# Last norm of a one-core hybrid decoder layer: a reordered finish, with the left output halves on GpSimd and ScalarE

## Chip, cores and metric

The kernel runs on one core of a Trainium2 chip. The metric is the device time in microseconds (us) of one execution. Engines are called by their names in the profile: PE (TensorE matmul), PEld (TensorE weight load), DVE (VectorE), ACT (ScalarE), POOL (GpSimd), SP (the engine that issues most DMAs).

## What is computed

One decoder layer over 512 tokens of width 1024: two mixing branches, a cross-attention, a mixture of 64 experts of which each token takes 8, and a last RMS norm. Only the end matters here:

```python
def rmsnorm(x, g):
    xf = x.astype(jnp.float32)
    y = xf * lax.rsqrt(jnp.mean(xf * xf, axis=-1, keepdims=True) + EPS)
    return (y * g.astype(jnp.float32)).astype(x.dtype)

    h = h + moe(rmsnorm(h, g_ffn[l]), ...)
return rmsnorm(h, g_final)
```

In `moe`, a token's output is the sum of its 8 expert rows, each times its gate, plus a shared expert's row (already in `h` when the end begins).

## The kernel before

All arithmetic is in float32. The 512 tokens are four tiles (`NT` = 4) of 128 partitions; `h[:, i, :]` in SBUF is tile `i`, 1024 wide. The expert rounds (44 of them) fill most of the time: weights stream from memory, PE multiplies, and POOL writes the rows of each round to a buffer in memory by indirect DMA.

The end begins when the last rounds are written. SP loads the 8 expert rows of each token back, as 16 transfers of 1024 KB: a "row pair" for each `q` of 0 to 3 and each tile `i` (`load_row_pairs`, L700 to L709). The pairs lie in the weight buffers that have come free (`ring`, `dw`, `z`). Each tile's 1024 columns are then summed in two halves by two engines:

- The right half (columns 512 to 1023) on PE: `sum_right_halves` (L1290) adds `h` and the 8 rows, each times a diagonal matrix of gates, into a PSUM bank `ps[:, i, :]`. The last pair of a tile raises `s_prs`. Between `q` = 1 and `q` = 2 PE also spreads the last norm's weight over the partitions (L1309), and ACT copies it to `gf` in SBUF (L1644).
- The left half (columns 0 to 511) on DVE: `add_rows` (L2286) for `q` 0 to 2 and `sum_last` (L2312) for `q` = 3, two `scalar_tensor_tensor` operations each, in place in `h`. `sum_last(i)` raises `s_red`.

ACT squares each half with a sum over the columns (L1647 left, L1649 right), and after tiles 1 and 3 takes a square root (`roots`, L1343) of the mean that DVE has made (`tile_squares`, L2294: an add, and `mean_square` at L1680). DVE makes the inverse root with one correction step (`tile_roots`, `inverse_root` at L1690: a reciprocal and four small operations, each waited for by `link`). `scale(i)` (L2304) multiplies both halves of tile `i` by the inverse root and by `gf`; each half raises `s_fin`. SP stores the eight halves, 256 KB each, in the order left 0, right 0, left 1, right 1, and so on (L736 to L740), each after its own count of `s_fin`, and waits for all of them at the end.

The order of each engine's work is its program order; nothing is reordered at run time. DVE's order at the end is written out in `sum_and_finish` (L2328 to L2338). POOL has nothing to do after its last indirect DMA. The tiles `h`, `z`, `ring`, `tok` and `st` lie in SBUF, `ps` in PSUM.

Of the kernel before, what the change touches and what calls it, by code (L numbers as in the profile page):

```python
# [21 lines left out]
ALU = mybir.AluOpType  # L22
ACT = mybir.ActivationFunctionType
# [6 lines left out]
D = 1024  # L30
S = 512
NT = S // P
# [14 lines left out]
EPS = 1e-6  # L47
# [11 lines left out]
PI_MAX = 3.1415925  # L59


C_ID, C_ONE, C_CAUSAL, C_FREQ, C_SLOT, C_BEFORE, C_FOLD, C_KEY = 0, 128, 192, 320, 352, 356, 420, 484
NCONST = 485
QW, NQ = 32, 4
FIXED, FULL, THREE = 4, 8, 24
NBUF = 6
# [84 lines left out]
def shape_constants():  # L151

    c = np.zeros((P, NCONST), np.float32)
    c[:, C_ID:C_ID + P] = np.eye(P)
    c[:, C_ONE:C_ONE + NE] = 1.0
    q, k = np.arange(P)[:, None], np.arange(P)[None, :]
    c[:, C_CAUSAL:C_CAUSAL + P] = np.where(k <= q, 0.0, -BIG)
    c[:, C_FREQ:C_FREQ + DQ // 2] = 10000.0 ** (-np.arange(0, DQ, 2) / DQ)
    for i in range(NT):
        c[:, C_SLOT + i] = S * TOPK - TOPK * (P * i + np.arange(P))  # L160
    a, b = np.arange(NG)[:, None], np.arange(NG)[None, :]
    c[:, C_BEFORE:C_BEFORE + NG * NG] = (b < a).astype(np.float32).ravel()
    c[:, C_FOLD:C_FOLD + NE] = np.tile(np.eye(NE), (2, 1))
    e = np.arange(NE)
    key = np.where(e < FIXED, -S * NE * 3 * (1 + e), NE - 1 - e)
    c[0:NE, C_KEY] = key
    late = np.zeros((P, NLATE), np.float32)
    for q in range(NQ):
        late[:, L_RANK + q * NR:L_RANK + (q + 1) * NR] = [RANK_AT[UNITS[r][1][q]] for r in BY_COL]
    late[:, L_KEY:L_KEY + NE] = key  # L170
    late[0:NE, L_EXP:L_EXP + QW] = e[:, None]
    return np.concatenate([c, late], axis=1)
# [11 lines left out]
def hybrid_layer(nc, t, consts, out):  # L184
# [5 lines left out]
    def sem(name):  # L190
        return ctx.enter_context(nc.semaphore(name))


    h = sb("h", [P, NT, D])
    tok = sb("tok", [P, NT * D])
    act_t = sb("act_t", [P, NC_D * S])
    z = sb("z", [P, NT * 2048])
    dw = sb("dw", [P, 3, 2048])
    ring = sb("ring", [P, 4, 6144])
    cst = sb("cst", [P, NCONST])  # L200
    pcol = sb("pcol", [P, NROWS])
    gcat = sb("gcat", [P, NC_D])
    st = sb("st", [P, 96])
# [13 lines left out]
    def view(base, off, *dims):  # L217

        n = int(np.prod(dims))
        v = base[:, off:off + n]  # L220
        names = "abcd"[:len(dims)]
        if len(dims) == 1:
            return v
        return v.rearrange("p (%s) -> p %s" % (" ".join(names), " ".join(names)),
                           **{k: d for k, d in zip(names, dims)})

    K = 256
# [43 lines left out]
    st2 = sb("st2", [P, 64])  # L271
# [63 lines left out]
    s_sq = sem("squares_ready")  # L335
    s_var = sem("variance_ready")
    s_sd = sem("deviation_ready")
    s_dev = sem("deviations_of_x_then_moe_ready")
    s_tf = sem("turned_filled")
    s_tea = sem("turned_evac_act")  # L340
    s_tev = sem("turned_evac_dve")
# [41 lines left out]
    s_oe = sem("attn_out_evac")  # L383
    s_osq = sem("attn_squares_ready")
    s_gin = sem("gelu_input_then_inner_ready")
    s_gst = sem("gelu_squares_ready")
    s_th = sem("tanh_ready")
    s_yg = sem("gelu_ready")
    s_ygt = sem("gelu_turned")
    s_yge = sem("gelu_turned_evac")  # L390
    s_gl = sem("gate_filled")
    s_sg = sem("gate_sigmoid_ready")
    s_y3 = sem("gated_ready")
    s_cat = sem("branches_ready")
    s_memn = sem("mem_normed")
# [55 lines left out]
    s_yl = [sem(f"rows_loaded{i}") for i in range(10)]  # L451
    s_red = sem("tile_rows_summed")
    s_prs = sem("half_rows_summed_pe")
    s_fin = sem("output_ready")
    s_out = sem("output_stored")


# [15 lines left out]
    tp = view(z, 0, NT, D)  # L473
    scr = view(z, 16 * K, 12, NT * NE)
    grow = view(ya, 0, D)
    rbias = view(ya, D, NE)
    wr = view(ya, D + NE, NC_D, NE)
    tv, ts_, row_of = view(tok, 3 * D, S), view(tok, 3 * D + S, SLOTS), view(tok, 3 * D + S + SLOTS, NE)
# [29 lines left out]
    yo = [view(z, (8 + b * 4) * K, D) for b in range(2)]  # L508

    gf_row = z[0:1, 0:D]  # L510
    gf, gf_spread = z[:, D:2 * D], ps[:, 6:8, :].rearrange("p a b -> p (a b)")
    LOADED = [[0, 0, 1, 1], [2, 2, 3, 3], [4, 4, 5, 5], [6, 7, 8, 9]]
    OF_LOAD = [sum(row.count(n) for row in LOADED) for n in range(10)]
# [81 lines left out]
    def _(sp):  # L595
# [140 lines left out]
        for i in range(NT):  # L736
            for n in range(2):
                cols = slice(n * 512, (n + 1) * 512)
                sp.wait_ge(s_fin, 2 * i + n + 1)
                sp.dma_start(out[0, i * P:(i + 1) * P, cols], h[:, i, cols]).then_inc(s_out, 16)  # L740
        sp.wait_ge(s_out, 16 * 2 * NT)

# [583 lines left out]
    def _(act):  # L1326
# [16 lines left out]
        def roots(n, a, b):  # L1343

            act.wait_ge(s_var, n)
            act.activation(st[:, b], st[:, a], ACT.Sqrt).then_inc(s_sd, 1)
# [288 lines left out]
        def norm_squares():  # L1635

            act.wait_ge(s_gk, NT * TOPK + 1)
            for q in range(4):
                for i in range(NT):
                    for k in range(2):  # L1640
                        act.activation(gate_diagonal(q, i, k), ident, ACT.Copy, scale=gate_of(q, i, k)).then_inc(s_dg, 1)
            act.activation(st2[:, 44:45], st2[:, 0:1], ACT.Sqrt)
            act.wait_ge(s_prs, 1)
            act.activation(gf, gf_spread, ACT.Copy).then_inc(s_dg, 1)  # L1644
            for i in range(NT):
                act.wait_ge(s_red, i + 1)
                act.activation(tok3[:, i, 0:512], h[:, i, 0:512], ACT.Square, accum_out=st[:, i:i + 1]).then_inc(s_sq, 1)  # L1647
                act.wait_ge(s_prs, 1 + i + 1)
                act.activation(tok3[:, i, 512:D], ps[:, i, :], ACT.Square, accum_out=st[:, 4 + i:5 + i]).then_inc(s_sq, 1)  # L1649
                if i % 2:  # L1650
                    roots(7 + i // 2, slice(i - 1, i + 1), slice(8 + i - 1, 8 + i + 1))

        with act.If(slots_needed(act) < 1):
            norm_squares()
# [7 lines left out]
    def _(dve):  # L1662
# [17 lines left out]
        def mean_square(var, width):  # L1680

            link(dve.tensor_scalar(var, var, 1.0 / width, EPS, ALU.mult, ALU.add))
            dve.sem_inc(s_var, 1)
# [610 lines left out]
        def tile_squares(a, b):  # L2294

            dve.wait_ge(s_sq, 18 + 2 * b)
            link(add(st[:, a:b], st[:, a:b], st[:, 4 + a:4 + b]))
            mean_square(st[:, a:b], D)

        def tile_roots(a, b):  # L2300

            inverse_root(7 + a // 2, st[:, a:b], st[:, 8 + a:8 + b], st2[:, a:b])

        def scale(i):  # L2304

            dve.wait_ge(s_dg, 2 * NT * 4 + 1)
            for n in range(2):
                cols = slice(n * 512, (n + 1) * 512)
                dve.scalar_tensor_tensor(out=h[:, i, cols], in0=ps[:, i, :] if n else h[:, i, cols], scalar=st2[:, i:i + 1],
                                         in1=gf[:, cols], op0=ALU.mult, op1=ALU.mult).then_inc(s_fin, 1)  # L2310

        def sum_last(i):  # L2312

# [8 lines left out]
        def sum_and_finish(loads):  # L2322

            dve.wait_ge(s_gk, NT * TOPK + 1)
            for q in range(3):
                for i in range(NT):
                    add_rows(q, i, loads, slice(0, 512))
            for i in range(3):  # L2328
                sum_last(i)
            tile_squares(0, 2)  # L2330
            tile_roots(0, 2)
            sum_last(3)
            scale(0)
            tile_squares(2, 4)
            scale(1)
            tile_roots(2, 4)
            scale(2)
            scale(3)  # L2338
# [25 lines left out]
    def _(pool):  # L2364
# [98 lines left out]
        with needs_passes(pool):  # L2463
            all_scattered(NR)
            with pool.Fori(0, PASSES) as p:
                pool.wait_ge(s_tab, p + 3)
                pool.sem_inc(s_zero, 1)
                one_pass(p)
            pool.sem_inc(s_rows, 1)

    ctx.close()

# [17 lines left out]
```

## Time and profile before

| | us |
|---|---|
| time, median of 3 runs | 1126.96 |
| lowest and highest run | 1123.72, 1128.65 |
| span of the profiled execution, first to last instruction | 1122.3 |
| PE busy | 1072.1 (96%) |
| DVE busy | 392.8 (35%) |
| ACT busy | 233.1 (21%) |
| POOL busy | 121.7 (11%) |

The span is of one execution, recorded by the profiler on the core. A busy share is an average over the whole span; the end, from about 1080 us on, is read from its own stretch. Positions in the trace are us from the start of the span. Rows of consecutive like instructions are merged in a timeline (x2, x3), and pipelined neighbours can overlap by up to 0.1 us.

### The profile page before, as it was taken

The numbers are of one execution on the slowest core, as the hardware profiler recorded it, in microseconds if no ns is written. First come the engines' busy times: TensorE is split into PE (matmuls) and PEld (weight loads), VectorE is DVE, ScalarE is ACT, GpSimd is POOL, SyncE is SP. The second block draws the span as 40 slices with busy tenths as digits, with TensorE's granted clock in tenths as the row PEclk, the third lists the DMA queues.
The fourth block names the chain that finished last, engine by engine and source line by source line (L and its number), as shares of the span: only waits on it lengthen the run. The fifth ranks groups of instructions, "written<-read, shape, count | busy, mean of one in ns | idle before, by whom it ended". The sixth has DMA issues, their size and how long they took to land.

```text
span 1122.3 us, 13366 instructions
## 1 busy us (share of the span) xinstructions
PE 1072.1 (96%) x5091; PEld 520.6 (46%) x5091; DVE 392.8 (35%) x924; ACT 233.1 (21%) x528; POOL 121.7 (11%) x187
## 2 busy tenths in 40 slices
PE   7999999989999999988899999999999998999996
PEld 4444687764444484443444433333344343443332
DVE  1894764553220040069322122122122121111157
ACT  4311523454111050031011111111111111111142
POOL 3000000000000000000211212211212211121100
PEclk9999999999999999999999999999999999999998
DMA  7225334221262502235699999999999999999997
GB/s 220 79 78 118 92 118 115 84 75 38 75 271 73 195 25 72 75 138 230 234 410 418 419 422 420 420 421 420 422 419 421 420 420 422 421 419 422 419 408 286
DMA packets 77346, 298.81 MB, mean 266 GB/s; under 512 B 20343, under 2 KB 23708, under 8 KB 50653
## 3 DMA queue, kind: packets, MB, share of 16 engines
q1 hardware_dynamic: 64386, 264.29, 60.1%
q0 software_dynamic: 12672, 33.57, 7.7%
q8 instruction: 42, 0.69, 0.2%
q14 instruction: 28, 0.22, 0.1%
q10 hardware_dynamic: 218, 0.04, 0.0%
HBM read 280.04 MB, written 27.39 MB: 274 GB/s over the span
## 4 chain that ended last, share of the span: by engine, by line
PE 87%; DVE 7%; ACT 2%; DMA 2%; issue 1%; DVEq 0%; SPq 0%; ACTq 0%
PE ps L1211 27%; PE ps L771 25%; PE ps L1227 14%; PE ps L1193 4%; PE ps L902 3%; PE ps L915 2%; PE ps L1300 2%; PE ps L1235 1%; DVE tok L2180 1%; DMA dw<-in_wv_x 1%; DVE tok L2177 1%; PE ps L1061 1%; PE ps L1080 1%; PE ps L951 1%; PE ps L752 1%
## 5 line engine op out<-in xcount | busy, mean ns | idle before, releaser
L1211 PE MATMUL ps<-ring,z 128*32 128x512 f32 (+2 forms) x1024 | 275.6, 594 | 0.7 <-DVE z L2228 0.5
L771 PE MATMUL ps<-dw,act_t 128*128 128x512 f32 x576 | 249.1, 593 | 1.3 <-ACT act_t L1518 1.0
L771 PEld LDWEIGHTS ps<-dw,act_t 128*128 128x128 f32 x576 | 108.8, 190 | 135.4 <-issue 133.5
L1227 PE MATMUL ps<-ring,act_t 128*32 128x512 f32 (+2 forms) x512 | 144.3, 607 | 4.5 <-issue 3.7
L1211 PEld LDWEIGHTS ps<-ring,z 128*32 128x32 f32 (+2 forms) x1024 | 87.7, 131 | 110.3 <-issue 108.2
L1211 PE MATMUL ps<-dw,z 128*64 128x512 f32 (+2 forms) x256 | 99.0, 594 | 2.1 <-issue 1.1
L1211 PE MATMUL ps<-z 128*32 128x512 f32 (+2 forms) x320 | 98.9, 594 | 0.0
L1604 ACT ACTIVATE tok<-ps 128x256 f32<-128x256 f32 x44 | 16.9, 383 | 299.8 <-PE ps L1211 299.8
L2208 DVE COPY z<-ps 128x512 f32<-128x512 f32 x44 | 30.4, 692 | 121.1 <-PE ps L1227 121.1
L1227 PEld LDWEIGHTS ps<-ring,act_t 128*32 128x32 f32 (+2 forms) x512 | 42.9, 133 | 55.1 <-issue 53.2
L1672 DVE TENSOR_TENSOR tok<-tok,ps 128x256 f32<-128x256 f32 x22 | 9.3, 421 | 151.2 <-ACT tok L1604 151.2
L1672 DVE TENSOR_TENSOR act_t<-tok,ps 128x256 f32<-128x256 f32 x22 | 9.3, 421 | 147.6 <-ACT tok L1604 147.6
L2374 POOL COPY ixb<-tabs 128x1 uint32<-128x1 uint32 x88 | 17.0, 193 | 375.2 <-DVE z L2208 361.9
L2443 POOL MEMSET act_t<- 128x1024 f32 x1 | 1.0, 952 | 510.1 <-PE ps L771 510.1
L771 PE MATMUL ps<-act_t,dw 128*128 128x512 f32 x128 | 55.2, 593 | 0.9 <-ACT act_t L1355 0.9
L1600 ACT ACTIVATE z<-ps 128x512 f32<-128x512 f32 x44 | 26.3, 597 | 137.9 <-PE ps L1227 137.9
L1227 PE MATMUL ps<-act_t 128*64 128x512 f32 (+2 forms) x128 | 50.9, 597 | 0.0
L1227 PE MATMUL ps<-dw,act_t 128*32 128x512 f32 (+2 forms) x160 | 50.9, 596 | 0.0
L2418 POOL DMA_INDIRECT expert_rows<-z,ixb x44 | 44.7, 1015 | 36.2 <-POOL ixb L2374 36.2
L1211 PEld LDWEIGHTS ps<-dw,z 128*64 128x64 f32 (+2 forms) x256 | 29.4, 132 | 33.7 <-issue 33.1
L1211 PEld LDWEIGHTS ps<-z 128*32 128x32 f32 (+2 forms) x320 | 29.9, 127 | 32.0 <-issue 31.3
L1193 PEld LDWEIGHTS ps<-cst,tok 128*128 128x128 f32 x264 | 32.5, 193 | 24.7 <-issue 24.7
(326 smaller groups left out, 1220.9 us busy)
## 6 DMA issues: line engine op xcount, KB each, us to landing
ring<-in_w_gate SPq DMA_DIRECT2D x40, 1024.0 KB
ring<-in_w_up SPq DMA_DIRECT2D x40, 1024.0 KB
ring<-in_w_down SPq DMA_DIRECT2D x40, 1024.0 KB, 26.8
dw<-in_w_gate SPq DMA_DIRECT2D x12, 1024.0 KB
dw<-in_w_up SPq DMA_DIRECT2D x12, 1024.0 KB
act_t<-in_w_down SPq DMA_DIRECT2D x12, 1024.0 KB, 24.6
z<-in_w_gate SPq DMA_DIRECT2D x12, 1024.0 KB, 19.9
z<-in_w_up SPq DMA_DIRECT2D x12, 1024.0 KB, 23.6
```

The lines of the kernel that those rows point to most:

```text
L771: ins = pe.matmul(ps[0:m, bank0 + j, 0:n], lhs(w, q * 4 + c4, c4, j), rhs(w, q * 4 + c4, c4, j), start=(q == 0 and c4 == 0), stop=(q == le ...
L902: ins = pe.matmul(ps[:, bank, 0:MEM], w4(dw[:, i % 3, :])[:, c4, j * P:(j + 1) * P], memt[:, hf * 4 + c4, :], start=(hf == 0 and c4 == 0), ...
L915: ins = pe.matmul(ps[:, bank, 0:256], memt[:, hf * 4 + c4, m * P:(m + 1) * P], w4(dw[:, i % 3, :])[:, c4, n * 256:(n + 1) * 256], start=(h ...
L1193: ins = pe.transpose(ps[:, c // 4, (c % 4) * P:(c % 4 + 1) * P], xg[r % 4][:, c:D:NC_D], ident)
L1211: ins = pe.matmul(ps[rows, 2 + r % 2, :], xtt[r % 2][:, c, rows], ring_wgu(BUF[x])[:, :, c, :], start=(c == 0), stop=(c == NC_D - 1))
L1227: ins = pe.matmul(ps[rows, 5 + n, :], htt[r % 2][:, c, rows], ring_wd(BUF[x])[:, c, n * 512:(n + 1) * 512], start=(c == 0), stop=(c == 1))
L1300: ins = pe.matmul(ps[:, i, :], gate_diagonal(q, i, k), row_pair(q, i)[:, k, 512:D], start=False, stop=(q == 3 and k == 1))
L1600: act.activation(yo[j % 2][:, 0:512], ps[:, 5, :], ACT.Copy).then_inc(e_yea, 1)
L1672: return dve.tensor_tensor(o, a, b, ALU.mult)
L2208: dve.tensor_copy(yo[j % 2][:, 512:D], ps[:, 6, :]).then_inc(e_yev, 1)
L2374: pool.tensor_copy(ixb[:, b:b + 1], tabs[:, which, col:col + 1] if isinstance(col, int) else tabs[:, which, bass.ds(col, 1)]).then_inc(s_p ...
L2418: pool.indirect_dma_start(yr, bass.IndirectOffsetOnAxis(ap=ixb[:, b:b + 1], axis=0), yo[r % 2], None, bounds_check=last_row, oob_is_err=Fa ...
```

## The change

Only the end of the kernel changes, and a constant that it needs.

1. DVE's order: `sum_last(3)` is put ahead of `tile_roots(0, 2)`, and `scale(1)` ahead of `tile_squares(2, 4)`.
2. `scale(i)` on DVE makes the right half alone. The left half becomes two steps. POOL multiplies `h[:, i, 0:512]` by `gf` into `left_products` as soon as `sum_last(i)` is done. ACT multiplies the product by the inverse root into `h`, all four tiles after its second square root.
3. `tile_squares`: the count that ACT's square root waits for is raised after the add; the mean is made beside it, and ACT takes scale and bias into the root (the new constant column `C_EPS`). `tile_roots`: a reciprocal and three operations in place of a reciprocal and four.
4. SP waits for ACT's count for left halves (`s_finl`) and DVE's count for right halves (`s_fin`). The order of the stores stays.

```diff
+c[:, C_EPS] = EPS          (NCONST 485 -> 486)
+    s_root, s_lp, s_finl = s_dev, s_gst, s_sg
+    left_products = view(z, 8 * K, NT, 512)
@@ SP
-                sp.wait_ge(s_fin, 2 * i + n + 1)
+                sp.wait_ge(*((s_fin, i + 1) if n else (s_finl, NT + i + 1)))
                 sp.dma_start(out[0, i * P:(i + 1) * P, cols], h[:, i, cols]).then_inc(s_out, 16)
@@ ACT, norm_squares
                 if i % 2:
-                    roots(7 + i // 2, slice(i - 1, i + 1), slice(8 + i - 1, 8 + i + 1))
+                    act.wait_ge(s_var, 7 + i // 2)
+                    act.activation(st[:, 8 + i - 1:8 + i + 1], st[:, i - 1:i + 1], ACT.Sqrt, scale=1.0 / D, bias=eps
+                                   ).then_inc(s_sd, 1)
+            for i in range(NT):
+                act.wait_ge(s_root, 3 + i // 2)
+                act.wait_ge(s_lp, NT + i + 1)
+                act.activation(h[:, i, 0:512], left_products[:, i, :], ACT.Copy, scale=st2[:, i:i + 1]).then_inc(s_finl, 1)
@@ DVE
             link(add(st[:, a:b], st[:, a:b], st[:, 4 + a:4 + b]))
-            mean_square(st[:, a:b], D)
+            dve.sem_inc(s_var, 1)
+            dve.tensor_scalar(st2[:, 40 + a:40 + b], st[:, a:b], 1.0 / D, EPS, ALU.mult, ALU.add)
         def tile_roots(a, b):
-            inverse_root(7 + a // 2, st[:, a:b], st[:, 8 + a:8 + b], st2[:, a:b])
+            r, near, mean = st2[:, a:b], st2[:, 32 + a:32 + b], st2[:, 40 + a:40 + b]
+            dve.wait_ge(s_sd, 7 + a // 2)
+            link(dve.reciprocal(r, st[:, 8 + a:8 + b]))
+            link(dve.scalar_tensor_tensor(out=near, in0=r, scalar=-0.5, in1=r, op0=ALU.mult, op1=ALU.mult))
+            link(mul(near, near, mean))
+            dve.scalar_tensor_tensor(out=r, in0=near, scalar=1.5, in1=r, op0=ALU.add, op1=ALU.mult).then_inc(s_root, 1)
         def scale(i):
             dve.wait_ge(s_dg, 2 * NT * 4 + 1)
-            for n in range(2):
-                cols = slice(n * 512, (n + 1) * 512)
-                dve.scalar_tensor_tensor(out=h[:, i, cols], in0=ps[:, i, :] if n else h[:, i, cols], scalar=st2[:, i:i + 1],
-                                         in1=gf[:, cols], op0=ALU.mult, op1=ALU.mult).then_inc(s_fin, 1)
+            dve.wait_ge(s_root, 3 + i // 2)
+            dve.scalar_tensor_tensor(out=h[:, i, 512:D], in0=ps[:, i, :], scalar=st2[:, i:i + 1], in1=gf[:, 512:D],
+                                     op0=ALU.mult, op1=ALU.mult).then_inc(s_fin, 1)
@@ DVE, sum_and_finish
             tile_squares(0, 2)
+            sum_last(3)
             tile_roots(0, 2)
-            sum_last(3)
             scale(0)
+            scale(1)
             tile_squares(2, 4)
-            scale(1)
             tile_roots(2, 4)
@@ POOL, at its end
+        pool.wait_ge(s_dg, 2 * NT * 4 + 1)
+        for i in range(NT):
+            pool.wait_ge(s_red, i + 1)
+            pool.tensor_tensor(left_products[:, i, :], h[:, i, 0:512], gf[:, 0:512], ALU.mult).then_inc(s_lp, 1)
```

## Rows read from the trace of the kernel before

**Rows 1.** The page: the chain that ended last, share of the span by engine.

```profile
PE 87%; DVE 7%; ACT 2%; DMA 2%; issue 1%; DVEq 0%; SPq 0%; ACTq 0%
```

**Rows 2.** Chain of work that ended last, from 1080 us: start, us, what.

```profile
1108.93 0.70 ACT tok L1649 x2
...
1112.91 0.72 ACT tok L1647 x2
...
1118.47 1.32 DVE h L2309 x2
```

**Rows 3.** Timeline, DVE: start, us, line op out<-in count [idle before <-releaser].

```profile
1103.69 1.54 DVE L2316 SCALAR_TENSOR_TENSOR h<-z,st,h 128x512 f32<-128x512 f32 x2
1105.44 1.54 DVE L2316 SCALAR_TENSOR_TENSOR h<-z,st,h 128x512 f32<-128x512 f32 x2 [0.21 <-DMA z<-expert_rows]
1107.93 1.54 DVE L2316 SCALAR_TENSOR_TENSOR h<-ring,st,h 128x512 f32<-128x512 f32 x2 [0.95 <-DMA ring<-expert_rows]
1109.65 0.16 DVE L1675 TENSOR_TENSOR st<-st 128x2 f32<-128x2 f32 x1 [0.18 <-ACT tok L1649]
...
1110.34 0.17 DVE L1694 RECIPROCAL st<-st 128x2 f32<-128x2 f32 x1 [0.33 <-ACT st L1346]
...
1111.33 1.54 DVE L2316 SCALAR_TENSOR_TENSOR h<-ring,st,h 128x512 f32<-128x512 f32 x2
1112.79 0.75 DVE L2309 SCALAR_TENSOR_TENSOR h<-h,st,z 128x512 f32<-128x512 f32 x1
1113.45 0.75 DVE L2309 SCALAR_TENSOR_TENSOR h<-ps,st,z 128x512 f32<-128x512 f32 x1
...
1116.08 0.15 DVE L1694 RECIPROCAL st<-st 128x2 f32<-128x2 f32 x1
```

**Rows 4.** Timeline, ACT, the square root and tile 3's squares.

```profile
1110.11 0.20 ACT L1346 ACTIVATE st<-st 128x2 f32<-128x2 f32 x1 [0.49 <-DVEq L1683]
...
1112.91 0.63 ACT L1647 ACTIVATE tok<-h 128x512 f32<-128x512 f32 x1 [1.41 <-DVE h L2316]
...
1113.54 0.58 ACT L1649 ACTIVATE tok<-ps 128x512 f32<-128x512 f32 x1
...
1114.01 0.19 ACT L1649 ACTIVATION_READ_ACCUMULATOR tok<-ps 128x1 f32 x1
```

**Rows 5.** Timeline, PEld: the wait for the last row pair.

```profile
1110.36 0.30 PEld L1300 LDWEIGHTS ps<-ring,act_t 128*128 128x128 f32 x2 [0.58 <-DMA ring<-expert_rows]
```

**Rows 6.** Timeline, SP: the eight stores, from first to last issue.

```profile
1113.56 6.58 SPq L740 DMA_DIRECT2D out<-h  x8
```

**Rows 7.** Windows: stretch, us, busy by engine, PEclk, DMA share, GB/s.

```profile
1114.00:1114.50 0.50, 0.00 (x0) 0.00 (x0) 0.43 (x3) 0.20 (x2) 0.00 (x0) 1.00 0.36 106
1118.50:1119.00 0.50, 0.00 (x0) 0.00 (x0) 0.50 (x1) 0.00 (x0) 0.00 (x0) 0.50 0.67 254
1120.00:1120.50 0.50, 0.00 (x0) 0.00 (x0) 0.00 (x0) 0.00 (x0) 0.00 (x0) 0.50 1.05 385
1121.00:1121.50 0.50, 0.00 (x0) 0.00 (x0) 0.00 (x0) 0.00 (x0) 0.00 (x0) 0.50 0.84 324
```

**Rows 8.** Timeline of 1079.8 to 1080.7 us, DVE and POOL.

```profile
1079.82 1.53 DVE L2291 SCALAR_TENSOR_TENSOR h<-ring,st,h 128x512 f32<-128x512 f32 x2
1080.04 0.56 POOL L2374 COPY ixb<-tabs 128x1 uint32<-128x1 uint32 x1 [2.97 <-DVE z L2208]
```

**Rows 9.** All 88 POOL copies of line 2374: ns min/median/max, first and last start.

```profile
L2374 POOL COPY ixb<-tabs x88: 177/183/562, 536.4 to 1080.0; 128x1 uint32<-128x1 uint32 x88
```

**Rows 10.** Timeline from 3 us: POOL and DVE at the kernel's start.

```profile
0.75 3.51 POOL L2366 MEMSET ring<- 128x4096 f32 x1 [0.29 <-POOLq L2478]
...
3.24 1.09 DVE L1728 COPY ring<-st 16x128 f32<-16x128 f32 x1 [3.24 <-DMA st<-in_log_dt]
```

**Rows 11.** DVE copies of 128x32: ns min/median/max, first and last start.

```profile
L1778 DVE COPY ring<-pw x8: 172/173/181, 38.2 to 38.8; 128x32 f32<-128x32 f32 x8
```

**Rows 12.** Groups by line, POOL: busy, mean ns of one, idle before.

```profile
L2443 POOL MEMSET act_t<- 128x1024 f32 x1 | 1.0, 952 | 510.1 <-PE ps L771 510.1
```

More of the change, by code:

```diff
@@ L59 @@
 PI_MAX = 3.1415925
-C_ID, C_ONE, C_CAUSAL, C_FREQ, C_SLOT, C_BEFORE, C_FOLD, C_KEY = 0, 128, 192, 320, 352, 356, 420, 484
-NCONST = 485
+C_ID, C_ONE, C_CAUSAL, C_FREQ, C_SLOT, C_BEFORE, C_FOLD, C_KEY, C_EPS = 0, 128, 192, 320, 352, 356, 420, 484, 485
+NCONST = 486
 QW, NQ = 32, 4
@@ L166, in shape_constants @@
     c[0:NE, C_KEY] = key
+    c[:, C_EPS] = EPS
     late = np.zeros((P, NLATE), np.float32)
@@ L337, in hybrid_layer @@
     s_sd = sem("deviation_ready")
-    s_dev = sem("deviations_of_x_then_moe_ready")
+    s_dev = sem("deviations_of_x_then_moe_then_output_ready")
     s_tf = sem("turned_filled")
@@ L385, in hybrid_layer @@
     s_gin = sem("gelu_input_then_inner_ready")
-    s_gst = sem("gelu_squares_ready")
+    s_gst = sem("gelu_squares_then_left_products_ready")
     s_th = sem("tanh_ready")
@@ L391, in hybrid_layer @@
     s_gl = sem("gate_filled")
-    s_sg = sem("gate_sigmoid_ready")
+    s_sg = sem("gate_sigmoid_then_left_output_ready")
     s_y3 = sem("gated_ready")
@@ L453, in hybrid_layer @@
     s_prs = sem("half_rows_summed_pe")
-    s_fin = sem("output_ready")
+    s_fin = sem("right_output_ready")
     s_out = sem("output_stored")
@@ L475, in hybrid_layer @@
     grow = view(ya, 0, D)
+    eps = cst[:, C_EPS:C_EPS + 1]
     rbias = view(ya, D, NE)
```

## The prediction

> **What bounds the kernel now.** I read the chain that ended last first. Over the whole span it is PE's, 87% of it [rows 1], and none of that is touched: up to about 1109 us PE multiplies while row pairs arrive. The change can act only on what follows. There the chain leaves PE at ACT's square of tile 1's right half, goes through tile 3's sum and squares, and ends in DVE's scalings [rows 2]. The last ends at 1118.47 + 1.32 = 1119.79 us. The span ends at 1122.3, so 2.5 us are the last stores.
>
> Next the DMA share in short windows, as the end is a store problem too. The first store is issued at 1113.56 [rows 6]; its half-microsecond window is busy for 0.36 x 0.5 = 0.18 us [rows 7], so data starts to flow at 1114.32, 0.76 us after the issue. The last four halves (left 2 to right 3) flow in one piece from 1119.00 - 0.67 x 0.5 = 1118.66 to 1121.00 + 0.84 x 0.5 = 1121.42, at a DMA share of 1.05 in the middle [rows 7]: 2.76 us for four, 0.69 us for each. DVE makes a half in 1113.45 - 1112.79 = 0.66 us [rows 3]. The two rates are nearly equal, so stores can hardly catch up on a late start. From the last byte (1121.42) to the end of the span it is 0.88 us. Eight stores back to back therefore cost 0.8 (issue to flow) + 8 x 0.69 + 0.88 = 7.2 us from the first issue. Before, 8.7 us lay between (1113.56 to 1122.3), with gaps of about 1.3 us.
>
> **What the first store will wait for.** SP's order stays: left 0 comes first, and everything stands behind it, right halves that have long been done too. Left 0 now comes from ACT, whose program has it behind the second square root. So the start of all stores hangs on tile 3. First without any contention:
> - The last row pair is there at 1110.36 [rows 5]. Before, DVE made tiles 0 and 1's roots first and summed tile 3 from 1111.33 to 1112.88. Now it sums from 1110.37: done at 1111.91, 0.97 us sooner.
> - The roots of tiles 0 and 1 follow. Five linked operations took 1111.33 - 1110.34 = 0.99 us, 0.2 each [rows 3]; four take 0.8: until 1112.71.
> - Right 0 and right 1, 0.66 us each, occupy DVE until 1114.05. Meanwhile ACT squares tile 3: from 1111.93, 1114.20 - 1112.91 = 1.29 us as before [rows 4], until 1113.22. It then waits for DVE, since the add of tiles 2 and 3 stands behind right 1. This is a wait that the new order makes: 0.8 us in which tile 3's squares lie ready.
> - Add 0.16 us, the count, square root 0.20: before, add start to root start was 1110.11 - 1109.65 = 0.46 us [rows 3, 4]; without the mean between, 0.26. The root ends at about 1114.52.
> - ACT's scaling of left 0. Its nearest row is the square of a left half in SBUF, 0.63 us [rows 4]; it ends at 1115.15.
>
> The first issue is then at 1115.17, against 1113.56 before: 1.6 us later. ACT needs about 0.6 us for each left half and a tile's two stores take 1.38, so the other left halves are in time (left 2 waits also for roots at about 1115.35, and is done before 1117). Right 3 is done at about 1116.75, 3 us sooner than before. Stores then run without a gap: 1115.17 + 7.2 = 1122.37. That is 0.1 us against the 1122.3 of before. All that compute gains goes into the later start.
>
> **What POOL's products cost.** They cost nothing on POOL, which is idle, and the fourth is wanted only some 2 us after left 0 is scaled. But POOL and DVE get in each other's way. One of POOL's 88 copies took 562 ns, median 183 [rows 9]. It started at 1080.04 and ended at 1080.60, just as the first of two DVE row sums ended, an operation with two SBUF inputs (1079.82 + 1.53/2 = 1080.58) [rows 8]. The other way round, a DVE copy of 16x128 took 1.09 us while POOL's memset ran, and ended at 4.33 where the memset ended at 4.26 [rows 10]; a DVE copy of 128x32 takes 0.17 [rows 11]. So each engine was seen waiting for the other's whole instruction. By the Trainium skill (SBUF — State Buffer, SBUF: two separate sides), the pair of ports that the two share is an exclusive lock: a GpSimd operation that reads SBUF and a VectorE operation with two SBUF inputs shut each other out for a full instruction. Both rows agree, though this pair of kinds with POOL ahead is not shown.
>
> I count as shut out what is of the kind of the row sums in [rows 8], with two inputs in SBUF: `sum_last`, the adds and three of the four root steps. The right halves read one input from PSUM and are counted free; so are the reciprocal and the mean, which have one input (if they are shut out too, as the copy of [rows 10], which also has one, that is up to 0.2 us more). The length d of a product stands in no row. POOL's nearest rows are memsets, which write only: 0.95 us for 128x1024 [rows 12], 3.51 for 128x4096 [rows 10], thus 0.83 ns an element. Lower bound: 512 elements at that rate with the fixed tenth, 0.5 us. Upper: three streams (two read, one written) of 512, 1.4 us. I take 0.95, two streams, the memset of 1024. (The Trainium skill, GPSIMD Engine Reference, Performance versus the Vector engine, has 4497 ns for 2048 elements of a two-input operation; by that an estimate of 1.1 us, and the sum below would be 0.6 us more.)
>
> With d = 0.95 and 0.14 us from a DVE end to a POOL start (before POOL's copy of 1080.04, DVE's previous operation ends at 1079.90):
> - product 0 holds until 1106.32, so tile 1's sum runs 1106.34 to 1107.88 instead of 1105.44 to 1106.98; this is hidden, as tile 2's rows arrive at 1107.93 [rows 3];
> - product 1 falls between the two operations of tile 2's sum: done 1110.40 instead of 1109.47;
> - product 2 starts behind the add at 1110.58 and holds until 1111.53; tile 3's sum ends at 1113.09 instead of 1111.91: 1.18 us;
> - product 3 starts at 1113.23, behind the reciprocal, and holds until 1114.18; the three other root steps follow: roots done 1114.79 instead of 1112.71, 2.08 us in all.
>
> Everything behind moves by these 2.08: first issue 1117.25, end 1124.45. Forecast: 1122.3 + 2.1 = 1124.4 for the span. The median of the runs (1126.96) stands 4.7 us above the profiled span, the fastest run 1.4; I carry the difference to the median over: 1126.96 + 2.1 = 1129.1 us. With d = 0.5 it is +0.5, with 1.4 +3.9 (roughly 3.9 us per us of d).
>
> The 486th constant column is 0.2% more of one early load; at most 0.02 us.
>
> **Rivals.**
> - No lock between these kinds. For: the rows show one pair of kinds in each direction, neither with POOL reading and ahead. Against: both show it. Then the sum without contention holds, 1122.4 for the span: 1127.0 us.
> - Not slower, and faster: compute bounds the end, not the stores. Place: SP's stores; they would have to flow quicker than 0.69 us each, or left 0 sooner. Then right 3 at 1116.75, plus 2.5 us: 1119.2, a gain of 3.1, 1123.9 us. Against: a share of 1.05 in the last burst [rows 7], and program order. It decides only where eight stores take under 2.4 us in all after 1115.17.
> - Clearly slower: products are long. From d = 0.95 + (5.6 - 2.1)/3.9 = 1.85 us on the loss is over 0.5% (1132.6 us); with d = 3, about 1137. Against: twice the memset of 1024 elements for half the elements.
>
> **Chances.** Forecast (lock, d 0.5 to 1.4) 0.58; no lock 0.24; compute-bound gain 0.07; long products 0.05; something outside the end, such as another course of the weight stream, 0.06. About 0.5% (5.6 us) is what a measurement can tell from no change: the three runs alone spread over 4.9 us. The whole stretch that changes is little longer, so within 0.5% holds 0.87. Over 0.5% slower: 0.09 (long products and the upper end of the forecast with the runs' spread). Over 0.5% faster: 0.04. Range: from 1124.0, the compute-bound case and the lower runs of no lock, to 1131.5, the forecast's upper bound (1130.9) with some spread.
>
> **What would show it.** Right: right 3 scaled well before its store; first store issue at about 1117.2, later than 1113.56, and then a DMA share near 1 without gaps for 5.5 us; DVE's tile sums showing gaps or long operations where POOL's products lie; POOL products of 0.5 to 1.4 us. Lock wrong: tile 3's sum ends at 1111.9 beside a running product, first issue 1115.2. Store bound wrong: gaps between stores with ACT late. The prediction fails if products take over 1.85 us, or if the time before 1105 us moves.

## The result, and the profile after

The changed kernel is a little slower: ratio to the kernel before 1.0027, 95% interval 1.0014 to 1.0040. Over 20 runs each, the medians are 1125.85 us and 1122.62 us. 0.27% of 1122.62 is 3.0 us (1.6 to 4.5).

The page of the changed kernel has the same shape; the chain's shares answer [rows 1]:

```profile
span 1122.6 us, 13377 instructions
...
PE 1072.9 (96%) x5091; PEld 520.8 (46%) x5091; DVE 393.3 (35%) x918; ACT 235.8 (21%) x532; POOL 127.7 (11%) x191
...
PE 87%; DVE 5%; DMA 3%; ACT 2%; issue 1%; SPq 0%; ACTq 0%; POOL 0%; POOLq 0%; DVEq 0%
```

The two spans, 1122.3 and 1122.6 us, hardly differ, and this is misleading: in the profiled execution of the changed kernel the whole end began 2.6 us sooner, since the streams of row pairs vary that much from one execution to the next. A common mark is needed. I take the start of DVE's sum of tile 1, which waits for that tile's last rows in every trace but follows no step of the change: 1105.44 before [rows 3], 1102.86 after. From this mark to the end of the span it is 16.86 us before and 19.74 after: 2.88 us longer, which is what the ratio says. The mark itself is good to about 0.35 us: two traces of one kernel differ by that much (below). The reason is PE, whose right halves come early or late against DVE's rows, so that DVE's add of tiles 0 and 1 starts 3.9 to 4.5 us after the mark in the traces where no product holds it up.

DVE's timeline of the changed kernel, which answers [rows 3]:

```profile
1101.09 1.54 DVE L2331 SCALAR_TENSOR_TENSOR h<-z,st,h 128x512 f32<-128x512 f32 x2
1102.86 2.53 DVE L2331 SCALAR_TENSOR_TENSOR h<-z,st,h 128x512 f32<-128x512 f32 x2 [0.22 <-DMA z<-expert_rows]
1105.34 2.43 DVE L2331 SCALAR_TENSOR_TENSOR h<-ring,st,h 128x512 f32<-128x512 f32 x2
1107.69 0.15 DVE L1685 TENSOR_TENSOR st<-st 128x2 f32<-128x2 f32 x1
1107.99 1.15 DVE L2309 TENSOR_SCALAR st<-st 128x2 f32<-128x2 f32 x1 [0.15 <-DVE st L1685]
1109.05 1.53 DVE L2331 SCALAR_TENSOR_TENSOR h<-ring,st,h 128x512 f32<-128x512 f32 x2
1110.49 0.16 DVE L2315 RECIPROCAL st<-st 128x2 f32<-128x2 f32 x1
1110.69 1.25 DVE L2316 SCALAR_TENSOR_TENSOR st<-st 128x2 f32<-128x2 f32 x1
...
1112.44 1.41 DVE L2324 SCALAR_TENSOR_TENSOR h<-ps,st,z 128x512 f32<-128x512 f32 x2
...
1115.21 1.41 DVE L2324 SCALAR_TENSOR_TENSOR h<-ps,st,z 128x512 f32<-128x512 f32 x2
```

POOL's timeline of the same stretch, which has no counterpart before:

```profile
1102.79 1.26 POOL L2488 TENSOR_TENSOR z<-h,z 128x512 f32<-128x512 f32 x1 [22.79 <-DVE h L2331]
1105.46 1.75 POOL L2488 TENSOR_TENSOR z<-h,z 128x512 f32<-128x512 f32 x1 [1.41 <-DVE h L2331]
1107.84 1.27 POOL L2488 TENSOR_TENSOR z<-h,z 128x512 f32<-128x512 f32 x1 [0.63 <-DVE h L2331]
1110.65 1.27 POOL L2488 TENSOR_TENSOR z<-h,z 128x512 f32<-128x512 f32 x1 [1.54 <-DVE h L2331]
```

Lay the two side by side. I say that POOL holds a DVE operation, or that a lock lies between them, where one stands still until the other is done. A product takes 1.26 us. The first starts at 1102.79, just ahead of tile 1's sum; the sum takes 2.53 us where 1.54 is its length. The second is asked for while the first operation of tile 2's sum runs: the product itself grows to 1.75 us (it waits for that operation), and the sum's second operation then waits for the product (2.43). The third holds the mean of tiles 0 and 1, a `TENSOR_SCALAR` of two columns: 1.15 us where 0.17 was. The fourth holds the second root step: 1.25 us where 0.16 was. The right halves from PSUM keep 1.41 us for two, but no product runs beside them here; the run with two of four products puts one there.

The chain that ended last shows the same places, and the ScalarE step that the stores wait for:

```profile
1107.99 1.15 DVE st L2309
...
1110.69 1.26 DVE st L2316
...
1114.21 0.93 ACT h L1661 x2
```

The stores (SP's timeline, then windows with DMA share and GB/s as the last two columns), which answer [rows 6, 7]:

```profile
1114.94 4.99 SPq L744 DMA_DIRECT2D out<-h  x8
```

```profile
1115.50:1116.00 0.50, 0.00 (x0) 0.00 (x0) 0.50 (x2) 0.50 (x2) 0.00 (x0) 0.50 0.40 152
1118.00:1118.50 0.50, 0.00 (x0) 0.00 (x0) 0.00 (x0) 0.00 (x0) 0.00 (x0) 0.50 1.01 389
1121.00:1121.50 0.50, 0.00 (x0) 0.00 (x0) 0.00 (x0) 0.00 (x0) 0.00 (x0) 0.50 0.56 213
```

The last half is computed at 1115.21 + 1.41 = 1116.62, but data flows from 1115.80 (1116.00 - 0.40 x 0.5) to 1121.28 (1121.00 + 0.56 x 0.5) without a gap: 5.48 us for eight halves. Computing ends 6.0 us before the span does; in the kernel before it was 2.5.

1121.28 is where the full flow ends, not the last byte. Windows of what follows, first after, then before:

```profile
1121.30:1121.80 0.50, 0.00 (x0) 0.00 (x0) 0.00 (x0) 0.00 (x0) 0.00 (x0) 0.50 0.09 33
1121.80:1121.90 0.10, 0.00 (x0) 0.00 (x0) 0.00 (x0) 0.00 (x0) 0.00 (x0) 0.50 0.01 0
1121.90:1122.60 0.70, 0.00 (x0) 0.00 (x0) 0.00 (x0) 0.00 (x0) 0.00 (x0) 0.50 0.00 0
```

```profile
1121.50:1121.60 0.10, 0.00 (x0) 0.00 (x0) 0.00 (x0) 0.00 (x0) 0.00 (x0) 0.50 0.02 0
1121.60:1122.30 0.70, 0.00 (x0) 0.00 (x0) 0.00 (x0) 0.00 (x0) 0.00 (x0) 0.50 0.00 0
```

In the changed kernel a trickle of packets of the stores' queue goes on until 1121.87, from 1121.4 on a packet every 0.08 us, where the share is near 1 in the full flow; from there to the end of the span it is 0.73 us. In the kernel before the last packet lies at 1121.55, just behind the full flow (1121.42), and the rest is 0.75 us.

### The profile page after: what moved, and what is told of

Read it like the earlier page. It is cut to its first block, busy times and chain, and to the rows that moved or that the text cites. A ratio compares the mean times of both kernels' runs of the same rounds, so it can differ in the third digit from the quotient of the medians.

```text
span 1122.6 us, 13377 instructions
## 1 busy us (share of the span) xinstructions
PE 1072.9 (96%) x5091; PEld 520.8 (46%) x5091; DVE 393.3 (35%) x918; ACT 235.8 (21%) x532; POOL 127.7 (11%) x191
## 4 chain that ended last, share of the span: by engine, by line
PE 87%; DVE 5%; DMA 3%; ACT 2%; issue 1%; SPq 0%; ACTq 0%; POOL 0%; POOLq 0%; DVEq 0%
PE ps L1215 27%; PE ps L775 27%; PE ps L1231 14%; PE ps L1197 4%; PE ps L906 3%; PE ps L919 2%; PE ps L1239 1%; DMA z<-expert_rows 1%; PE ps L756 1%; DVE tok L2190 1%; DVE tok L2187 1%; PE ps L1065 1%; PE ps L955 1%; PE ps L1084 1%; DMA dw<-in_wv_x 1%
```

## The experiments

The theory: (a) POOL's products and DVE's operations shut each other out (the lock), which delays left 0; (b) the end is then set by eight stores in a row behind their late start. The rivals: the loss comes from the new order alone; computing sets the end. Some runs leave out, shorten or replace the products, others store only half of each half: their output is not the layer's, and only their times are used.

All results in one table. "Offset" is the time in the trace from the mark (start of tile 1's sum on DVE), first to the first store's issue and then to the end of the span; its difference to the kernel before (16.86) stands beside the ratio from the timed runs, each with 95% interval.

| kernel | ratio to before | first issue | end | end against before |
|---|---|---|---|---|
| before | | 8.12 | 16.86 | |
| changed | 1.0027 (1.0014 to 1.0040) | 12.08 | 19.74 | +2.88 |
| no products | 1.0007 (0.9996 to 1.0019) | 9.74 | 17.19 | +0.33 |
| before, with products | 1.0020 (1.0005 to 1.0035) | 9.81 | 18.88 | +2.02 |
| left 0 and 1 ahead of the second root | 1.0017 (1.0003 to 1.0031) | 10.22 | 17.96 | +1.10 |
| the same without products | 1.0005 (0.9990 to 1.0019) | 8.53 | 16.89 | +0.03 |
| products of 256 columns | 1.0013 (1.0000 to 1.0027) | 10.54 | 18.11 | +1.25 |
| changed, stores of 256 columns | 1.0011 (0.9994 to 1.0029) | 12.07 | 17.65 | +0.79 |
| before, stores of 256 columns | 0.9994 (0.9978 to 1.0009) | 7.79 | 16.14 | -0.72 |
| two of four products | 0.9998 (0.9979 to 1.0018) | 6.28 | 15.75 | -1.11 |
| two of four, again | 1.0004 (0.9983 to 1.0025) | 6.80 | 16.10 | -0.76 |
| two of four, squares first | 0.9988 (0.9965 to 1.0011) | 6.86 | 16.18 | -0.68 |
| memsets for products | 1.0000 (0.9971 to 1.0028) | 9.74 | 17.27 | +0.41 |
| copies for products | 1.0000 (0.9976 to 1.0024) | 10.13 | 17.79 | +0.93 |

0.1% is 1.1 us. The intervals are as wide as most effects here; the offsets carry the readings, and every offset lies within its ratio's interval.

**Without the products.**

```diff
-            pool.tensor_tensor(left_products[:, i, :], h[:, i, 0:512], gf[:, 0:512], ALU.mult).then_inc(s_lp, 1)
-                act.wait_ge(s_lp, NT + i + 1)
-                act.activation(h[:, i, 0:512], left_products[:, i, :], ACT.Copy, ...)
+                act.activation(h[:, i, 0:512], h[:, i, 0:512], ACT.Copy, ...)
```

> The changed kernel without GpSimd's four products; ScalarE scales the left half of h itself, so the weight of the last norm is left out of the left output halves. Lock theory: the long VectorE records (1.75 and 1.64 us where 0.78 was before, 1.15 and 1.26 where 0.17) are gone, tile 3's left sum ends 1.55 us after its rows are there, the first store is issued 4.8 us after that arrival, eight stores take 7.2 to 7.7 us from there; the time is 3 us under the changed kernel, ratio to the kernel before 0.999 to 1.001. Rival (the loss comes from the order alone, GpSimd costs nothing): time as the changed kernel, ratio 1.0027. Rival (compute bounds the end): 3 us under the kernel before, 0.997.

DVE's timeline of this run:

```profile
1105.21 1.54 DVE L2330 SCALAR_TENSOR_TENSOR h<-z,st,h 128x512 f32<-128x512 f32 x2 [0.22 <-DMA z<-expert_rows]
1107.70 1.54 DVE L2330 SCALAR_TENSOR_TENSOR h<-ring,st,h 128x512 f32<-128x512 f32 x2 [0.94 <-DMA ring<-expert_rows]
1109.54 0.16 DVE L1684 TENSOR_TENSOR st<-st 128x2 f32<-128x2 f32 x1 [0.30 <-ACT tok L1653]
```

Every long record is gone, the first issue comes 2.34 us sooner (12.08 to 9.74), the end 2.55. So the products cause the long records and most of the loss; the order alone is no explanation, since it leaves 0.33 us. Nor is there the gain of the compute-bound rival: all that the change saves in computing is lost to the later start of the stores, as the next runs show.

**The kernel before, with the products beside it.** POOL's four products are added to the kernel before; nothing uses them.

```diff
+        pool.wait_ge(s_dg, 2 * NT * 4 + 1)
+        for i in range(NT):
+            pool.wait_ge(s_red, i + 1)
+            pool.tensor_tensor(left_products[:, i, :], h[:, i, 0:512], gf[:, 0:512], ALU.mult).then_inc(s_gst, 1)
@@ DVE, scale
+            dve.wait_ge(s_gst, NT + i + 1)
```

> The kernel before with the four GpSimd products beside it; their results are used by nothing, VectorE only waits for product i before it scales tile i in place. Lock theory: each product of 1.26 us stretches a VectorE operation with two SBUF inputs by about a product's rest; product 0 is hidden up to 0.3 us, the others cost 0.5 to 1.2 us each: 2 to 3.5 us slower than before, ratio 1.002 to 1.003. Rival (GpSimd costs nothing): ratio 1.000, every row sum of VectorE 0.75 us long.

2.2 us by the ratio, 2.02 by the offset. In the old order, too, the products by themselves cost about as much as the whole change lost (2.88). Their hold falls on the same kinds: DVE's timeline has the mean of two columns at 1.26 us, and the add of tiles 2 and 3 at 0.44:

```profile
1110.43 1.26 DVE L1683 TENSOR_SCALAR st<-st 128x2 f32<-128x2 f32 x1
...
1115.91 0.44 DVE L1676 TENSOR_TENSOR st<-st 128x2 f32<-128x2 f32 x1
```

**Left halves of tiles 0 and 1 ahead of the second root.**

```diff
@@ ACT, behind tile 3's squares, ahead of the second root
+                if i == 3:
+                    for m in range(2):
+                        act.wait_ge(s_root, 3 + m // 2)
+                        act.wait_ge(s_lp, NT + m + 1)
+                        act.activation(h[:, m, 0:512], left_products[:, m, :], ACT.Copy, scale=st2[:, m:m + 1]).then_inc(s_finl, 1)
```

> The changed kernel, but ScalarE scales the left halves of tiles 0 and 1 ahead of the second square root instead of behind it. Store theory (the start of the first store sets the end): left 0 is done 0.65 us after the first roots instead of 2.5 us after them, the first issue comes 1.9 us sooner, and as the stores then run without a gap the time falls by up to 1.9 us against the changed kernel: ratio to the kernel before 1.001. The second root moves by at most 0.3 us. Rival (the last computed half sets the end): no gain or a loss up to 0.3 us, ratio 1.0027.

First issue 1.86 us sooner, end 1.78 sooner, with the last half computed as late as in the changed kernel (right 3 at 1118.37, which is 13.73 after the mark, against 13.76). The start of the stores sets the end, not the last computed half.

**The same without products.** Both edits together.

> Both at once: no GpSimd products (the last norm's weight left out of the left output halves) and the left halves of tiles 0 and 1 scaled ahead of the second square root. Lock and store theory: the gains add, 4.9 us under the changed kernel and 1.9 us under the kernel before, ratio 0.998; the first store is issued 3.0 us after the last rows are there. Rival (stores do not bound): as the run without products alone.

The expectation was missed. The end is 0.30 us sooner than without products alone, not 1.9. The first issue gained 1.21, not 1.9: without the lock the first roots are ready at 1111.63, while ACT squares tile 3 until 1112.30. And the stores no longer ran in one piece (windows, DMA share second to last):

```profile
1114.00:1115.00 1.00, 0.00 (x0) 0.00 (x0) 0.78 (x5) 0.37 (x1) 0.00 (x0) 1.00 0.97 365
1115.00:1115.50 0.50, 0.00 (x0) 0.00 (x0) 0.50 (x2) 0.50 (x2) 0.00 (x0) 1.00 0.50 176
1115.50:1116.00 0.50, 0.00 (x0) 0.00 (x0) 0.50 (x1) 0.46 (x1) 0.00 (x0) 0.70 0.13 37
1116.00:1117.00 1.00, 0.00 (x0) 0.00 (x0) 0.12 (x1) 0.00 (x0) 0.00 (x0) 0.50 0.98 369
```

SP's timeline has the issue of the third store, left 1, at 1.61 us, where 0.45 is the median of the eight:

```profile
1113.89 1.61 SPq L744 DMA_DIRECT2D out<-h  x1
```

So a gap of 0.7 us opened in the stream. It wasn't computing that was late: left 1 was done at 1112.30 + 1.32 = 1113.62, and the fourth store, right 1, done at 1113.16, was issued only at 1115.55, behind the long issue. Why one issue takes so long stays open; the longest of the eight is 0.34 to 1.61 us over these traces, and a gap shows only where the stores have nothing queued.

**Products of 256 columns.**

```diff
-            pool.tensor_tensor(left_products[:, i, :], h[:, i, 0:512], gf[:, 0:512], ALU.mult)
+            pool.tensor_tensor(left_products[:, i, 0:256], h[:, i, 0:256], gf[:, 0:256], ALU.mult)
```

> The changed kernel with GpSimd products of 256 columns in place of 512; the last norm's weight is left out of the output columns 256 to 511. Lock theory: a product takes 0.65 to 0.7 us instead of 1.26, and each VectorE operation that it holds up is 0.6 us shorter; three products are on the path and one is half hidden, so 2.0 us (1.7 to 2.3) under the changed kernel, ratio to the kernel before 1.001. Rival (a fixed cost for each GpSimd operation, such as its start or its semaphores): no less than 1.002.

A product takes 0.72 us, and the held root step follows it:

```profile
1110.41 0.71 DVE L2316 SCALAR_TENSOR_TENSOR st<-st 128x2 f32<-128x2 f32 x1
```

The end is 1.63 us sooner than in the changed kernel by the offset, 1.6 by the ratio: just under what was expected. The cost goes with the product's length: first issue 9.74, 10.54 and 12.08 us after the mark with products of 0, 0.72 and 1.26 us. It is not a straight line, since short holds hide behind the arrival of rows: tile 2's come 2.5 us after the mark, tile 3's 4.9.

**Stores of half the width**, in the changed kernel and in the kernel before.

```diff
+                half = slice(n * 512, n * 512 + 256)
-                sp.dma_start(out[0, i * P:(i + 1) * P, cols], h[:, i, cols]).then_inc(s_out, 16)
+                sp.dma_start(out[0, i * P:(i + 1) * P, half], h[:, i, half]).then_inc(s_out, 16)
```

> The changed kernel, but each of the eight stores moves 256 of its 512 columns; the other columns of the output are not written. Store theory: the changed kernel's end is bound by 1 MB more of stores behind a late start; with half the bytes the eight take 4.5 us from the first issue instead of 7.7, 3.2 us (2.7 to 3.3) under the changed kernel, ratio to the kernel before 0.9995 to 1.000. Rival (computing bounds the end): 0.4 us less, ratio 1.0023.

> The kernel before, with each store moving 256 of its 512 columns; the other columns of the output are not written. Store theory: before, the last computed half sets the end, and only its own store gets shorter: 0.3 to 0.5 us less, ratio 0.9996. Rival (its stores bound it as well, since four run back to back at the end): 1.4 us less, ratio 0.9987.

The changed kernel gains 2.09 us by the offset (1.8 by the ratio), the kernel before 0.72, of which 0.33 lie ahead of the first issue and so not in the stores (8.74 to 8.35 us from there: 0.39, as expected); there DVE's add doesn't wait for ACT, as it did for 0.18 us before. The direction is clear in the offsets, while the ratio of the kernel before, for itself, doesn't tell a gain from none: the changed kernel is bound by its stores, the kernel before is not. The size of the first was wrong, 2.09 for 3.2. From first issue to end it is 5.58 us, not 4.5. SP's timeline says why:

```profile
1115.42 3.77 SPq L745 DMA_DIRECT2D out<-h  x8
```

Eight issues take 3.77 us, 0.47 each, more than the 0.35 us in which I had half a store flow. With halves this small it is SP's issuing that sets the pace.

**Two of four products.** A version made from these findings. POOL multiplies tile 0's left half (beside a wait for rows) and tile 3's (beside two right halves from PSUM). DVE makes left 1 and left 2 itself. ACT scales left 0 ahead of tile 3's squares. The cut leaves out ACT's part and the body of `scale_left`.

```diff
@@ POOL
-        for i in range(NT):
+        for i in (0, 3):
@@ DVE, sum_and_finish
             tile_squares(0, 2)
-            sum_last(3)
             tile_roots(0, 2)
+            sum_last(3)
             scale(0)
             scale(1)
+            scale_left(1)
             tile_squares(2, 4)
             tile_roots(2, 4)
             scale(2)
+            scale_left(2)
             scale(3)
@@ SP
-        for i in range(NT):
-            for n in range(2):
+        for i, n, done, count in ((0, 0, s_finl, NT + 1), (0, 1, s_fin, 1), (1, 1, s_fin, 2), (1, 0, s_fin, 3),
+                                  (2, 1, s_fin, 4), (3, 0, s_finl, NT + 2), (2, 0, s_fin, 5), (3, 1, s_fin, 6)):
```

> A version made from the findings: GpSimd multiplies the left halves of tiles 0 and 3 alone, tile 0's where VectorE waits for rows and tile 3's while VectorE makes two right halves from PSUM; VectorE makes the left halves of tiles 1 and 2 itself; ScalarE scales left 0 ahead of tile 3's squares; roots of tiles 0 and 1 ahead of tile 3's sum; stores in the order in which halves get done. Lock and store theory: first issue 6.8 us after tile 1's last rows instead of 8.1, last half done 12.3 us after them instead of 14.35; 1.5 to 2.0 us under the kernel before, ratio 0.9985. If right halves are held up by a GpSimd product too: the two right halves beside tile 3's product take over 1.9 us instead of 1.4, and the ratio is 0.9995 or more.

> The version with two of the four GpSimd products once more, for its interval: by the offsets of its trace it should be 1.1 us under the kernel before, ratio 0.999. If the two are equal, as its first runs also allow, 1.000.

The two traces put it 1.11 and 0.76 us ahead of the kernel before, the ratios (0.9998 and 1.0004) call it equal. The computing came out as planned, the first issue at 6.28 us, the last half at 12.11. The product beside right halves holds nothing (DVE, then POOL, of the first of the two runs):

```profile
1113.56 1.40 DVE L2334 SCALAR_TENSOR_TENSOR h<-ps,st,z 128x512 f32<-128x512 f32 x2
```

```profile
1113.72 1.27 POOL L2500 TENSOR_TENSOR z<-h,z 128x512 f32<-128x512 f32 x1 [5.57 <-DVE h L2341]
```

But the gain of 1.6 us at the first half of tile 2 (1117.74 is 10.79 after the mark; left 2 before was at 12.37) reached the end by only 1.1, as the end came 4.96 us after it instead of 4.49. The trickle behind the full flow explains most of that: its last packet lies at 1121.95, 0.75 us ahead of the end, while the full flow ends at about 1121.4. The two runs of this one kernel differ by 0.35 us from the mark: that is how good the mark is, as PE's and DVE's progress shift against each other (DVE's add waits 0.41 us for ACT in the second run and not at all in the first).

**Squares first.** The same, with `tile_squares(2, 4)` ahead of `scale_left(1)`.

> The version with two of the four GpSimd products, with VectorE's add and mean of tiles 2 and 3 ahead of the left half of tile 1, so that ScalarE's second root runs beside that half. The final four stores set the end by their start: the first half of tile 2 is done 0.3 to 0.4 us sooner after tile 1's last rows (10.4 instead of 10.8 us), the end 15.4 us after them instead of 15.75, against 16.86 in the kernel before: ratio to it 0.9985 to 0.999. If the landing of the last store grows with the queue in front of it, no gain over the other order: 0.999.

No gain: 16.18 us, against 15.75 and 16.10 of the other order. Right 2 is done 11.29 us after the mark, exactly as in the second run of the other order. The root's wait went, but the add now waits for ACT's squares. So no version beats the kernel before by more than its interval. By the offsets the three traces are 0.7 to 1.1 us better, which is two or three times what the mark is good for; against the changed kernel two of four products is 3.6 to 4.0 us better by the offsets, 2.6 to 3.3 by the ratios.

**What kind of POOL operation holds what.** The products replaced by a memset that reads nothing, or by a copy of one input. With memsets, ACT scales `h` itself, and each memset also waits for the one before; the cut leaves both out.

```diff
-            pool.tensor_tensor(left_products[:, i, :], h[:, i, 0:512], gf[:, 0:512], ALU.mult).then_inc(s_lp, 1)
+            pool.memset(view(z, 8 * K, 1536), 0.0).then_inc(s_lp, 1)          (first kernel)
+            pool.tensor_copy(left_products[:, i, :], h[:, i, 0:512]).then_inc(s_lp, 1)    (second kernel)
```

> The changed kernel with each GpSimd product replaced by a memset of 128x1536 (1.3 us, written to a free place, nothing read); ScalarE scales h itself, the last norm's weight is left out of the left output halves. If the lock needs a GpSimd operation that reads SBUF: VectorE's row sums of two inputs keep 0.75 us each and the first store is issued 9.7 us after tile 1's last rows, ratio as without products, 1.0007; only single-input operations such as the mean could be held. If any GpSimd operation holds the pair: row sums of 1.6 to 1.75 us as with the products, first issue at 12 us, ratio 1.0027.

> The changed kernel with each GpSimd product replaced by a copy of the left half of h (one input, no weight: it is left out of the left output halves). If a copy takes 0.5 to 0.6 us, one stream, VectorE is held for as long in each case and the time lies between the version without products and that with products of 256 columns: first issue 10.0 to 10.5 us after tile 1's last rows, ratio 1.001. If VectorE is held only by operations of two inputs: first issue 9.7 us, 1.0007.

With memsets, POOL and then DVE:

```profile
1103.23 1.38 POOL L2488 MEMSET z<- 128x1536 f32 x1 [23.06 <-DVE h L2330]
...
1107.41 1.38 POOL L2488 MEMSET z<- 128x1536 f32 x1 [1.11 <-DVE h L2330]
```

```profile
1103.33 1.54 DVE L2330 SCALAR_TENSOR_TENSOR h<-z,st,h 128x512 f32<-128x512 f32 x2 [0.21 <-DMA z<-expert_rows]
...
1107.76 1.06 DVE L2308 TENSOR_SCALAR st<-st 128x2 f32<-128x2 f32 x1 [0.15 <-DVE st L1684]
```

Tile 1's sum runs beside a memset at its usual 1.54 us, so a POOL operation that only writes does not hold a DVE operation of two inputs. The mean, of one input, does not end until the memset does (1107.41 + 1.38 = 1108.79, and the mean ends at 1108.82). But DVE is not held up by it: the next sum starts at 1108.26, inside the mean's record, 4.93 us after the mark and so when tile 3's rows are there, and takes its usual 1.54:

```profile
1108.26 1.54 DVE L2330 SCALAR_TENSOR_TENSOR h<-ring,st,h 128x512 f32<-128x512 f32 x2
```

A long record is thus not yet a cost. The first issue is at 9.74 us as without products.

With copies, the first issue is at 10.13 us, inside what was expected for the lock, and each copy takes 0.61 us. DVE is held in three places, for less: tile 1's sum (1.87 us), the mean and a root step; tile 2's rows come only as the second copy ends (1106.45 + 0.61 = 1107.06, the sum starts at 1106.96), and tile 2's sum keeps 1.54. The ratios of these two runs, from ten executions each, are too wide to tell anything (DVE's timeline with copies):

```profile
1104.51 1.87 DVE L2331 SCALAR_TENSOR_TENSOR h<-z,st,h 128x512 f32<-128x512 f32 x2 [0.21 <-DMA z<-expert_rows]
...
1108.72 0.47 DVE L2309 TENSOR_SCALAR st<-st 128x2 f32<-128x2 f32 x1 [0.15 <-DVE st L1685]
...
1111.06 0.57 DVE L2316 SCALAR_TENSOR_TENSOR st<-st 128x2 f32<-128x2 f32 x1
```

This is the rule of the Trainium skill (SBUF — State Buffer, SBUF: two separate sides): against an operation of two SBUF inputs only a GpSimd operation that reads SBUF counts, against one that runs in a mode of two ports any does. The traces agree with the first part. They agree with the second if the mean ran in such a mode, which no run shows by itself.

## Why the prediction was right, and where not

**What failed** are sizes, not the path. Four steps of the prediction were off, each with its number below: the length of a product (0.95 us, measured 1.26), what a hold costs (the whole product, measured 0.89 to 1.09 us of its 1.26), the constant tail of the stores (7.2 us, measured 7.66), and the base and noise on which the change was set (1126.96 us with 0.5% as the least that can be told, measured 1122.62 us with an interval of 0.13%).

**The mechanism was right.** Its likeliest case, the lock, is what happened, and so is the store theory: first issue later than before although right 3 was ready sooner, then one gapless burst. Slower by 2.1 us was forecast, 3.0 (1.6 to 4.5) measured; "within 0.5%" held.

**The sum without contention** was nearly exact. It had the first issue at 1115.17, which is 9.73 us after the mark; the run without products has 9.74. Its end was forecast 0.1 us over the kernel before and lies 0.33 over it.

**The length of a product** was the first mis-sized term: 0.95 us taken from POOL's memset of 1024 elements, 1.26 measured, within the bounds of 0.5 and 1.4. The estimate of 1.1 from the Trainium skill (GPSIMD Engine Reference, Performance versus the Vector engine) was nearer and still low.

**What the products cost on the way to the first store**: 2.08 us forecast, 12.08 - 9.74 = 2.34 measured. That so much longer a product cost only 0.26 us more is luck: a second error offsets the first. By the forecast's own slope of 3.9 us per us of product, 1.26 would have cost about 3.3. The forecast let each hold cost the whole product; the rows of the changed kernel show 0.99, 0.89, 0.98 and 1.09 us. Against the run without products they add up so: the first is hidden, as tile 2's sum starts 2.48 us after the mark here and 2.49 there, when its rows come. The second and third, 1.87 together, delay tile 3's sum by 1.27 (it starts at 6.19 us instead of 4.92), as without products the add waits 0.30 us for ACT, and tile 3's rows come only then (with copies the profile names that wait, and the sum starts at 4.90). The fourth delays the roots by its whole 1.09. That makes 2.36, against the 2.34 measured.

**"The mean has one input and is counted free"** was wrong: it was held for 0.98 us. It cost little beyond the sum because the third product would otherwise have held tile 3's sum, as the prediction had it, and the run with memsets shows DVE going on past a held mean. The prediction's own [rows 10] had warned: there a copy of one input stood still beside a memset. That row was read as agreeing with a lock between two-input and reading operations, but it is another pair of kinds, and in the run with memsets a sum of two inputs is not held by a memset. The right halves from PSUM were free, as assumed.

**The constant tail** was the other mis-sized term. "Eight stores back to back cost 7.2 us" came out as 19.74 - 12.08 = 7.66. The flow was right (5.48 us for 5.52). From the end of the full flow to the end of the span it was 1.32 us instead of 0.88. The prediction called this the time from the last byte, which it is not: from the last packet to the end it is 0.73 us here, 0.75 before and 0.71 without products. What grew is the trickle behind the full flow, from 0.13 us to 0.59 (0.39 without products). Together: 0.27 us from the first issue (12.08 - 8.12 = 3.96 against 3.69) and 0.46 from the tail make 0.73, the whole of 2.88 against 2.15 (1124.45 - 1122.3). A smaller slip: the 8.7 us of before were said to hold gaps of 1.3 us, while 8.7 - 7.2 leaves 1.5.

**The absolute time** of 1129.1 us was 3.3 too high although the change was forecast too small: it stood on a median of three runs, 1126.96, and over 20 runs the kernel before has 1122.62. And a difference of 0.5% was called the least that can be told; with 20 runs the interval is 0.13% to either side, and 0.27% stands clear of zero. The change of 2.1 us itself lies inside the measured 1.6 to 4.5.

**The rivals.** No lock is refuted by every trace with products. Compute-bound is refuted by the run with left 0 and 1 ahead of the root, and by the stores of half width. It holds for the kernel before, whose end hardly moves with half the bytes (0.39 us from the first issue). In the run of both edits it was not computing but a slow issue that made the gap. Long products did not occur.

## What to carry to other kernels

Moving an elementwise step to an idle GpSimd isn't free if VectorE works on SBUF operands at the time: each product held VectorE for about 1 us to save it 0.66, and only products beside a wait for data or beside VectorE work that reads PSUM were free. When the last results go out through one ordered queue, look at when its first entry is ready and at the bytes behind it, not at when the last result is computed. Executions that differ by several us in an untouched part need a common mark before two traces are compared. And an instruction whose record grows costs time only if the next one starts later for it.

## What was not expected of the hardware

- A VectorE operation of two columns and one input (`TENSOR_SCALAR`, 0.17 us alone) was held until the GpSimd operation beside it ended: 1.15 us beside a product, 1.06 beside a memset, 0.47 beside a copy. Its two columns were no shelter. Beside the memset the next VectorE operation started all the same, 0.56 us before the held one ended.
- GpSimd's product of two SBUF inputs took 1.26 us for 128x512 and 0.72 for 128x256, its copy 0.61 for 128x512, its memset 1.38 for 128x1536. When asked for during a VectorE operation of two inputs it took 1.75, waiting first.
- From the last packet of the stores to the end of the span it took 0.7 to 0.8 us in every trace read for it. Ahead of that packet, a trickle behind the full flow lasted 0.13 us in the kernel before, 0.39 without products, 0.59 in the changed kernel, and about 0.55 in the first run of two of four products, whose last burst has four stores as before. Why it varies, no run here tells.
- One store's issue took 1.61 us on SP in one trace, against a median of 0.45 there. This stays open too.
